# A two-block transformer kernel: Fourier product by halves, and waits, loads and steps put in another order

## Time and profile before

| what | value |
|---|---|
| median of three runs | 2947.27 us (2946.25 to 2950.39) |
| the profiled execution | 2950.16 us, span 2948.4 us |
| TensorE busy | 2840.2 us, 96% of the span |
| VectorE busy | 1644.5 us, 56% |
| ScalarE busy | 1124.3 us, 38% |
| mean granted TensorE clock | 0.987 |
| weights loaded | 391.43 MB by SyncE's queue |

### The profile page before, as it was taken

One profiled execution on the slowest core, in us unless ns is written; L12 is line 12 of the kernel. 1 busy time (PEld: TensorE's weight loads), 2 busy tenths in 40 slices (PEclk: granted clock), 3 DMA queues, 4 the chain that ended last, 5 costly groups with the idle time before them and its releaser, 6 DMA issues.

```text
span 2948.4 us, 44779 instructions
## 1 busy us (share of the span) xinstructions
PE 2840.2 (96%) x16592; PEld 2370.8 (80%) x16592; DVE 1644.5 (56%) x2829; ACT 1124.3 (38%) x1715; POOL 48.1 (2%) x36
## 2 busy tenths in 40 slices
PE   7999999999999999999999999999999998999998
PEld 7759998659998888785666778888788887788998
DVE  6547656447666555677334476555533336745665
ACT  4345534345542222324544232222322223584443
POOL 0100001000000000030000000000000000000000
PEclk9999999999999999999999999999999999999999
DMA  5574554655544343321221233433322222234454
GB/s 186 182 247 144 184 182 130 221 210 196 185 157 145 140 150 128 121 91 40 76 68 54 96 112 139 149 133 132 105 94 98 91 96 98 89 112 144 164 183 152
DMA packets 118357, 400.08 MB, mean 136 GB/s; under 512 B 12896, under 2 KB 20960, under 8 KB 117856
## 3 DMA queue, kind: packets, MB, share of 16 engines
q1 hardware_dynamic: 115120, 391.43, 39.1%
q10 hardware_dynamic: 3120, 7.07, 0.7%
HBM read 397.40 MB, written 1.05 MB: 135 GB/s over the span
## 4 chain that ended last, share of the span: by engine, by line
PE 84%; DVE 6%; DMA 3%; ACT 3%; issue 2%; DVEq 1%; POOL 1%; SPq 0%; ACTq 0%; POOLq 0%
PE bank L812 23%; PE bank L815 22%; PE bank L818 22%; PE bank L2234 4%; DMA ring<-weights 3%; PE bank L1534 2%; DVE w_lo L773 1%; PE bank L1979 1%; PE bank L1959 1%; DVE hn_lo L1019 1%; DVE work L2048 1%; PE bank L899 1%; ACT w_hi L749 1%; PE bank L1463 1%; POOL w_lo L773 1%
## 5 line engine op out<-in xcount | busy, mean ns | idle before, releaser
L773 DVE TENSOR_TENSOR w_lo<-ring,w_hi 128x1024 fp32r<-128x1024 f32 (+1 forms) x538 | 650.0, 1209 | 720.8 <-ACT w_hi L749 718.5
L749 ACT ACTIVATE w_hi<-ring 128x1024 fp32r<-128x1024 f32 (+1 forms) x548 | 571.4, 1044 | 1172.5 <-DMA ring<-weights 1172.2
L815 PE MATMUL bank<-hn_hi,w_hi 128*128 128x256 f32 (+1 forms) x2816 | 885.1, 334 | 0.0
L818 PE MATMUL bank<-hn_lo,w_hi 128*128 128x256 f32 (+1 forms) x2816 | 884.6, 334 | 0.0
L815 PEld LDWEIGHTS bank<-hn_hi,w_hi 128*128 128x128 f32 x2816 | 536.9, 191 | 52.2
L818 PEld LDWEIGHTS bank<-hn_lo,w_hi 128*128 128x128 f32 x2816 | 536.8, 191 | 52.2
L812 PE MATMUL bank<-hn_hi,w_lo 128*128 128x256 f32 (+1 forms) x2816 | 559.0, 341 | 15.0 <-DVE w_lo L773 5.6
L812 PEld LDWEIGHTS bank<-hn_hi,w_lo 128*128 128x128 f32 x2816 | 445.5, 191 | 84.7 <-issue 19.8
L815 PE MATMUL bank<-hid_hi,w_hi 128*128 128x512 f32 (+1 forms) x704 | 248.7, 363 | 0.0
L818 PE MATMUL bank<-hid_lo_a,w_hi 128*128 128x512 f32 (+1 forms) x640 | 226.2, 363 | 0.0
L812 PE MATMUL bank<-hid_hi,w_lo 128*128 128x512 f32 (+1 forms) x704 | 156.8, 363 | 4.9 <-DVE work L2160 4.9
(11 more groups left out here) (320 smaller groups left out, 3006.3 us busy)
## 6 DMA issues: line engine op xcount, KB each, us to landing
ring<-weights SPq DMA_DIRECT2D x692, 512.0 KB, 3.3
ring<-weights SPq DMA_DIRECT2D x32, 384.0 KB, 3.0
ring<-weights SPq DMA_DIRECT2D x32, 256.0 KB, 2.6
ring<-weights SPq DMA_DIRECT2D x28, 192.0 KB, 2.3
con<-consts ACTq DMA_DIRECT2D x1, 2063.0 KB, 7.4
con<-consts ACTq DMA_DIRECT2D x1, 1088.0 KB, 5.0
res<-ctx_cm ACTq DMA_DIRECT2D x1, 1024.0 KB, 14.1
con<-params ACTq DMA_DIRECT2D x1, 1024.0 KB, 7.1
```

The costliest lines, as they stand in the source:

```text
L749: act.activation(w_hi[:, slot, 0:w], ring[slot][:, 0:w], ACT.Copy).then_inc(s.w_hi, 1)
L773: eng.tensor_tensor(w_lo[slot][:, 0:w], ring[slot][:, 0:w], w_hi[:, slot, 0:w].bitcast(F32), ALU.subtract).then_inc(s.w_lo, 1)
L815: pe.matmul(dst, high, x_hi(k), start=False, stop=False)
L818: mm = pe.matmul(dst, high, x_lo(k), start=False, stop=(stop and k == order[-1]))
```

## The change

In the second Fourier product the cosine part is formed for positions 0 to 128 only (129 columns) and the sine part for 1 to 127 (127 columns); both lie side by side in the bank. ScalarE copies columns 0 and 128 to the result and the sine part to a buffer; VectorE adds for positions 1 to 127 and subtracts, written backwards, for 255 to 129. It does so behind taps 23, 24, 26 and 28, and only then is the bank free. The latent means go behind the second Fourier step on TensorE, the roots behind the third copy on ScalarE. Further: the first low split of lat_in goes ahead of the last wait in conv_in (layer 1); the wait of `ffn_pe` and the one ahead of mix_out are gone, and mix_out's first product goes row by row; the constants' load is issued right behind the first split, the context's load behind the second norm of layer 0; and in in_t the recurrence's step goes ahead of the split.

```diff
+FOUR_TAP = {23: 0, 24: 1, 26: 2, 28: 3}
...
+            if by_row and g.at == 0:
+                for k in order:
+                    low_pass(k)
+                    mm = high_passes(k)
+            else:
+                for k in order:
+                    low_pass(k)
+                for k in order:
+                    mm = high_passes(k)
...
                 first_split(split_high, act, PLAN["in_t", 0])
+                act.dma_start(con12[:, 0:CONST_SETS[1][1]], consts[1]).then_inc(s.consts1, 16)
             norm_act(act, 2 * l, PLAN["in_t", l], PLAN["down", l - 1] if l else None)
             if l == 0:
-                act.dma_start(con12[:, 0:CONST_SETS[1][1]], consts[1]).then_inc(s.consts1, 16)
-                act.dma_start(res[:, :, T:2 * T], ctx_cm).then_inc(s.ctx_in, 16)
...
             norm_act(act, 2 * l + 1, PLAN["up", l], PLAN["wo", l])
+            if l == 0:
+                act.dma_start(res[:, :, T:2 * T], ctx_cm).then_inc(s.ctx_in, 16)
...
             for m in range(lin.n):
-                splits_ahead(split_low, dve, lin, Group(m, m, 0, period(1)))
                 if m == SLOT_F and l == 0:
                     dve.wait_ge(s.consts1, 16)
                 hg_dve(dve, l, m)
+                splits_ahead(split_low, dve, lin, Group(m, m, 0, period(1)))
...
             gated_pair(pe, lin, n, w)
-            wait_all_drained(pe, lin)
...
+            for n, (u, stage, a, tt, gp) in enumerate(fourier_steps(l)):
+                if n == 2:
+                    latent_means(pe, l)
...
                     for c in range(seqs(l)):
-                        for i in range(4):
-                            mm = pe.matmul(b[:, c * T:(c + 1) * T],
-                                           f1[:, c, i // 2, a, (i % 2) * P:(i % 2 + 1) * P],
-                                           dft_t[:, i // 2, i % 2, :], start=(i == 0), stop=(i == 3))
+                        for part, (k0, k1) in enumerate(((0, P + 1), (1, P))):
+                            at = c * T + (P + 1) * part
+                            for t2 in range(TT):
+                                mm = pe.matmul(b[:, at:at + k1 - k0], f1[:, c, t2, a, part * P:(part + 1) * P],
+                                               dft_t[:, t2, part, k0:k1], start=(t2 == 0), stop=(t2 == TT - 1))
...
         def fourier_act(act, l):
+            for n, (u, stage, a, tt, gp) in enumerate(fourier_steps(l)):
+                if n == 3:
+                    latent_rstd(act, l)
...
-                    act.activation(four[:, a, 0:seqs(l) * T], b[:, 0:seqs(l) * T], ACT.Copy).then_inc(s.f_sb, 1)
+                    src = both(b, seqs(l) * T)
+                    act.activation(both(four[:, a, :], seqs(l) * T)[:, :, 0:P + 1:P], src[:, :, 0:P + 1:P], ACT.Copy)
+                    act.activation(sine_half(l, a), src[:, :, P + 1:T], ACT.Copy).then_inc(s.f_half, 1)
...
+        def fourier_dve(dve, l, a):
+            u = fourier_steps(l)[-G4 + a][0]
+            dve.wait_ge(s.f_half, G4 * l + a + 1)
+            src = both(bank[4 + u % 2], seqs(l) * T)[:, :, 1:P]
+            dst = both(four[:, a, :], seqs(l) * T)
+            dve.tensor_tensor(dst[:, :, 1:P], src, sine_half(l, a), ALU.add)
+            dve.tensor_tensor(dst[:, :, T - 1:P:-1], src, sine_half(l, a), ALU.subtract).then_inc(s.f_sb, 1)
...
-            wait_all_drained(pe, PLAN["mrg_mla", l])
             lin = PLAN["mix_out", l]
...
-                              lambda k: mrg_hi[:, k, 0:w], lambda k: mrg_lo[:, k, 0:w])
+                              lambda k: mrg_hi[:, k, 0:w], lambda k: mrg_lo[:, k, 0:w], by_row=True)
...
             for g in turns(dve, lin, tail=2):
-                splits_ahead(split_low, dve, lin, g)
+                splits_ahead(split_low, dve, lin, g, PLAN["lat_in", l] if seqs(l) == 1 else None)
...
             dve.drain()
-            if seqs(l) == 1:
-                first_split(split_low, dve, PLAN["lat_in", l])
             for k in range(CONV_K):
...
+                if k in FOUR_TAP:
+                    fourier_dve(dve, l, FOUR_TAP[k])
```

More of the change, by code:

```diff
@@ L525, in __init__ @@
         self.f_sb = sem("f_sb")
+        self.f_half = sem("f_half")
         self.sig_g = sem("sig_g")
@@ L800, in wait_split, with split_product @@
             pe.wait_ge(s.w_lo, split_number(lin, g, lin.split.index(c)) + 1)
-        def split_product(pe, lin, g, c, dst, wait_part, x_hi, x_lo, start=True, stop=True, order=None):
+        def split_product(pe, lin, g, c, dst, wait_part, x_hi, x_lo, start=True, stop=True, order=None, by_row=False):
             wait_split(pe, lin, g, c)
@@ L808, in split_product, with low_pass @@
             order = order or range(lin.tiles[c])
-            for k in order:
+            def low_pass(k):
                 if g.at == 0:
@@ L812, in split_product, with high_passes @@
                 pe.matmul(dst, w_lo[slot][:, k * P:(k + 1) * P], x_hi(k), start=(start and k == order[0]), stop=False)
-            for k in order:
+            def high_passes(k):
                 high = w_hi[:, slot, k * P:(k + 1) * P]
@@ L817, in split_product @@
                     wait_part(1, k)
-                mm = pe.matmul(dst, high, x_lo(k), start=False, stop=(stop and k == order[-1]))
-            mm.then_inc(used[slot], 1)
+                return pe.matmul(dst, high, x_lo(k), start=False, stop=(stop and k == order[-1]))
+            if by_row and g.at == 0:
[7 more added lines that the diff above has]
+                    mm = high_passes(k)
+            mm.then_inc(used[slot_of(lin, g, c)], 1)
         def normed_hi(w):
@@ L2190, in fourier_steps, with latent_means @@
             return [(u0 + n,) + x for n, x in enumerate(steps)]
+        def latent_means(pe, l):
+            w = seqs(l) * T
+            pe.wait_ge(s.c_sq, l + 1)
+            for k in range(3):
+                mm = pe.matmul(bank[6][:, 0:w], const(2, "ones_ct"), q2[:, 3 + k, 0:w], start=(k == 0), stop=(k == 2))
+            mm.then_inc(s.c_ms, 1)
+            for k in range(2):
+                mm = pe.matmul(bank[7][:, :], const(2, "ones_kv"), q2[:, 6 + k, :], start=(k == 0), stop=(k == 1))
+            mm.then_inc(s.c_ms, 1)
         def fourier_pe(pe, l):
             wait_all_drained(pe, PLAN["lat_in", l])
-            for u, stage, a, tt, gp in fourier_steps(l):
+            for n, (u, stage, a, tt, gp) in enumerate(fourier_steps(l)):
+                if n == 2:
+                    latent_means(pe, l)
                 b = bank[4 + u % 2]
@@ L2305, in block2_pe @@
                 input_product(pe, lin, g, 0, bank[2 * parity(lin, g)][:, 0:wg], n + 1, wg)
[L2307 to L2313, removed]
             fourier_pe(pe, l)
@@ L2423, in block2_act @@
             act.preload_act_table_set(LOG_EXP)
[L2424 to L2427, removed]
-                last = act.activation(tmp3[:, i, 0:wi], tmp3[:, i, 0:wi], ACT.Exp, scale=-0.5)
-            last.then_inc(s.c_rs, 1)
             fourier_act(act, l)
```

11 lines of the change are left out of this document (10 added, 1 removed).

## The result

The changed kernel took 2918.41 us in the median (2913.22 to 2921.08, four runs; the profiled execution 2915.96, span 2914.2), where the kernel before took 2948.1 on the same chip: a ratio of 0.9897, 95% interval 0.9879 to 0.9914. Run again later (a_again) it took 2920.2 against 2944.36: 0.9914, interval 0.9898 to 0.9929. So it gains 24 to 30 us; 24.7 was forecast, and the 2922.6 of the forecast lies 4 us above the first median and 2 above the second.

The account below looks back on a forecast made before the run. TensorE, at 84% of the span, was taken as the bound. Savings of 4.9, 4.9, 8.0, 3.2, 2.8 and 1.4 less 0.5 sum to 24.7 us: 2947.27 becomes 2922.6, range 2916.5 to 2933.5.

Parts of the forecast that it names:

- Start of the first layer: First norm and in_t, layer 0: earlier weight load and recurrent step ahead of the split save 8.0 us together.
- Second layer's in_t: in_t of layer 1: TensorE's idle of 3.09 us goes, with a little slow running behind it; 3.2 us saved.
- Hand-overs: Gated to output product, four feed-forwards: removing the wait for drained banks saves all 4.9 us of four waits.
- mix_out: Wait ahead removed and first product by row: 4.4 us saved in layer 0, 0.5 in layer 1, 4.9 together.
- Layer 0's Fourier part: Mixing, layer 0: halved second Fourier product saves 2.8 us; bounds 0 and, if the banks cost nothing, 4.
- Layer 1's mixing: Earlier lat_in split gains 4.9 us, roots lose 1.4, additions 1.9; 1.4 saved, bounds -3 and +1.5.
- The context's load: Load moved behind the second norm of layer 0: may overlap the next weight load, costing 0.5 us.
- (a): Start gives only its half; the two in_t terms bring 4 us instead of 11.2: 2930 us, chance 0.20.
- (b): Halved Fourier product gains nothing, bound by weight loads of 0.19 us each; layer 0 gives 0: 2925.4 us, chance 0.10.
- (c): Neither banks nor taps limit layer 0; the halved Fourier product yields all of 6.8 us: 2918.6 us, chance 0.08.
- (d): Removed waits at the four feed-forward hand-overs only move to the last row of hidden values: 2927.5 us, chance 0.05.
- (e): Short idles in layer 0's Fourier stretch drop the clock to 1.2 GHz: slower, 2950 to 2975 us, chance 0.02.

Follow-up runs that it names:

- e1: Changed kernel with the constants and the context loaded behind the first norm again, as before: 2924.81 us, 0.9932.
- e2: Changed kernel with the low split ahead of the recurrence's step in in_t again, both layers: 2929.96 us, 0.995.
- e5: Changed kernel with the second Fourier product over all 256 positions again, no additions on VectorE, latent means at their new place: 2923.53 us, 0.9925.
- v1: Changed kernel with latent means and roots ahead of the Fourier steps, halves in layer 0 only, whole product in layer 1: 2917.26 us, 0.9906.
- e4: Changed kernel with the latent means and their roots ahead of the Fourier steps and copies again, as before: 2917.75 us, 0.9905.
- e3: Changed kernel with the wait for all drained banks between gated and output product of the four feed-forwards back: 2925.52 us, 0.9937.
- e6: Changed kernel with the first low split of lat_in in layer 1 behind the last wait of conv_in again: 2923.62 us, 0.9923.
- e7: Changed kernel with mix_out's first product doing all low passes ahead of the high ones, the wait ahead still removed: 2920.92 us, 0.9921.

## Why the forecast was right

The total and its sign hold, and the range held both medians of the changed kernel. The closeness of the total is in part luck: by stretches the gain is 28, the terms for in_t of layer 1 and the hand-overs were too small, the one for the mixing of layer 1 too large, and 2.7 us came where nothing was forecast (the attention of layer 1, and a load in the merging). By its own terms:

- **Start of the first layer: right in sum (8.0 and 8.0), its parts not.** The prediction gave the load 3.3, the products behind it 0.4 net, and the step 4.3. Each undone alone costs 5.3 to 5.5, since it leaves an idle of 3 us or more and the slow clock behind that, 2.6 us of it in e1, where I had put 1.8. The wait at product 5, 1.4 by the forecast, is 0.61.
- **Second layer's in_t: undersized** (3.2 forecast; 4.8 to 5.3 in in_t itself, by e2 and by the means). The idle of 3.09 us was priced, the slow products behind it hardly: the 48 that follow the recurrence's product took 7.12 to 7.43 us before and take 5.95 now, and the recurrence's first product 1.09 instead of 1.6. Some 0.7 of it is lost again to the clock in the projections behind, which makes the table's 4.6.
- **Hand-overs: undersized by 0.8.** I counted the four idles (4.9) and not what surrounds them. Around an idle of 1.27 us the distance from start to start was 1.66 instead of 0.23, and the 24 products behind it took 0.12 longer.
- **mix_out: layer 0 right** (4.4 and 4.2), with the order worth 1.9 of it. **Layer 1 right too, with a load on top** (0.5 and 1.3). Of the 1.3 only 0.5 arises at mix_out. The other 0.8 arises 26 us ahead of it, in the merging, where no edit was made: in the three traces of before ScalarE waits 3.8 to 3.9 us there for a piece of weights and TensorE idles 0.5 to 0.6 (first two lines), in ten of the eleven changed traces it waits 2.6 to 2.9 and TensorE doesn't idle (third line). The eleventh, e5, has the wait of 3.83 and the 0.8 us again (167.74 against 166.90). Why the load lands later there stays open.

```profile
2687.89 1.06 ACT L749 ACTIVATE w_hi<-ring 128x1024 fp32r<-128x1024 f32 x1 [3.89 <-DMA ring<-weights]
2690.26 0.39 PE L812 MATMUL bank<-hn_hi,w_lo 128*128 128x256 f32 x1 [0.56 <-DVE w_lo L773]
```

```profile
2655.31 1.06 ACT L751 ACTIVATE w_hi<-ring 128x1024 fp32r<-128x1024 f32 x1 [2.94 <-DMA ring<-weights]
```

- **Layer 0's Fourier part: right where the clock holds** (2.8 forecast; 134.72 - 131.82 = 2.9 in three traces), 1.8 where it falls behind the idle of 1.90 us at L2224. There the steps hold too: TensorE runs out of banks for 1.90 us (2 forecast), VectorE's taps end 2.7 us later after the latent norm (2.7), and VectorE then waits 0.77 us for TensorE's mean (0.7), where it was 5.18. Where the clock falls, VectorE also waits 0.6 to 0.9 us for ScalarE's first copy. One bound was wrong: -4 "if the banks cost nothing". In v1 they cost nothing, and the gain is 2.9, since TensorE then waits for the first additions.
- **Layer 1's mixing: three effects right, the sum short** (1.4 and 0.2 to 0.5). The additions cost 2.0 (1.9 forecast), the roots 1.55 to 1.59 (1.4; the forecast's own times, 2532.49 less 4.9 against 2529.2, make it 1.6). The first split gave 4.07 us up to the latent norm (69.77 us after the start of conv_in before, 67.29 - 1.59 after), not 4.9: VectorE's idle spells shrank from 6.4 to 3.6 us (0.64, 2.16 and 0.78 are left), by 2.8 where I had put 3.7. The Trainium skill, VectorE: DVE Perf Modes, section on the TRN2 errata, gives a fp32 tensor_tensor (N + 151) cycles at 0.96 GHz, by estimate 0.29 us for 127 columns. The trace agrees with 0.28 for one addition. But the second starts 0.20 us behind the first, and the eight cost 2.0, not the 2.3 of an estimate by that page.
- **The context's load** cost nothing that can be seen; 0.5 had been put down.
- **The rivals.** (a), half of the start, is ruled out by e1, e2 and the repeats; (b) by 0.116 us an instruction; (c), no bound but TensorE, by the 2.9 us of layer 0 and by e4 and v1, where TensorE waits 2.8 us for a bank; (d) by e3. (e), the slow clock, did appear behind one idle in half of the traces, and costs 1.1 us there; over the 67 us that the forecast named the granted clock was 0.97, above its sign of 0.95. The forecast had it that the four idles of up to 1.3 us cost nothing behind them; they cost 0.1 each.

## What to carry to other kernels

Halving a product pays only where its engine sets the pace; the same edit is worth 2.9 us in the layer that TensorE bounds (5.2 with the latent means in their new place) and costs 2.0 in the one that VectorE bounds, so choose it per layer. Test each edit of a group in both settings of its neighbour: the means' new place went in with the halves, earned nothing in layer 0 and cost 1.55 us in layer 1. Ask of every helper instruction that an edit adds which engine's slack it eats, and place it where its input is just ready: one tap earlier moved a 2.85 us wait to 0.63. And price an idle of TensorE of 2 us or more with the slow products behind it: where the clock fell, they nearly doubled the loss in e1 (2.75 us of idle, 5.3 in all), and it did not fall every time.

## What was not expected

**The clock behind the same idle differs from run to run.** In eight traces TensorE idles 1.90 us at L2224 in layer 0. In four (the changed kernel, a_again, e3, e6) the clock falls behind it: the second Fourier product starts 5.0 to 5.3 us after that idle. In the other four (e1, e2, e5, e7) it stays at 1.00, and the second Fourier product starts after 3.7. Of the seven with the halves, the stretch of layer 0 takes 132.53 to 133.14 us with the fall and 131.78 to 131.86 without: 1.1 us in the mean. Windows of the changed kernel, then e1:

```profile
1324.43:1329.00 4.57, 4.54 (x12) 3.37 (x12) 4.57 (x8) 1.63 (x3) 0.00 (x0) 0.63 0.00 0
```

```profile
1335.01:1338.00 2.99, 2.94 (x12) 2.11 (x12) 2.99 (x6) 1.63 (x4) 0.00 (x0) 1.00 0.00 0
```

Longer idles did not settle it either. Behind 2.37 us ahead of lat_in in layer 1 the clock fell in all three traces of before (0.53 over 3.6 us in the first) and stayed at 1.00 in e6; behind 2.8 us in layer 0 it fell in e4 and stayed in v1. Counted over all fourteen traces, for idles that began at full clock: it fell behind 123 of 152 idles of 2 to 3 us, and behind none of 79 of 1.0 to 1.5 us. What decides in between is not shown.

**The same in the norms.** The ten us from the end of the last norm on have a clock of 0.83 in the first trace and 0.66 in a_again, e4, e6, e7 and v1, with the same waits of 0.4 us in them; up to lat_in the first, second, fourth and fifth of them take 0.9 to 1.1 us longer than the changed kernels with 0.83 (in e6 the wait ahead of lat_in comes on top). Windows of the changed kernel and of e6:

```profile
2433.59:2443.59 10.00, 8.39 (x51) 7.79 (x51) 5.59 (x10) 2.39 (x3) 0.00 (x0) 0.83 0.36 113
```

```profile
2439.33:2449.33 10.00, 8.58 (x42) 7.89 (x43) 5.59 (x10) 2.39 (x3) 0.00 (x0) 0.66 0.32 105
```

**Loads scatter by microseconds.** TensorE's waits for weights in the attention of layer 0 were 1.6 us in the first trace of the changed kernel and 4.3 in a_again, with the same program. That stretch is 6.1 us longer in a_again, of the 8.5 between the two traces. Whether the 8 us between the first four runs of the changed kernel come from there is not shown, since only one of them has a trace.
